# Sample rows routed ahead of the last output tile, and a new order of work up to the expert loop

## What is computed

```
x  <- LN1(alpha*x + y @ w_out)                    y: the two gated branches, merged
aff = sigmoid(x @ w_router)                       16 experts in 4 groups of 4
group g = argmax over groups of the sum of its two best (aff + b_router)
eid = the two best experts of group g;  wts = aff[eid] / sum(aff[eid])
h   = silu(xs @ w_gate[e]) * (xs @ w_up[e])       xs: the tokens of expert e, D_EXPERT = 512
x  <- LN2(alpha*x + sum over the two experts of wts * (h @ w_down[e]))
```

## Time and profile before

| | |
|---|---|
| median of 3 runs | 1908.78 us (1908.35 to 1909.92) |
| profiled execution, span | 1907.2 us |
| PE busy | 1856.5 us (97%) |
| DVE, ACT, POOL busy | 1164.8, 917.4, 481.8 us |
| w_out's last matmul ends | 1407.98 us |
| first round of the expert loop | 1462.02 us |

### The profile page before, as it was taken

One profiled execution on the slowest core, in us unless ns is written; L12 is line 12 of the kernel. 1 busy time (PEld: TensorE's weight loads), 2 busy tenths in 40 slices (PEclk: granted clock), 3 DMA queues, 4 the chain that ended last, 5 costly groups with the idle time before them and its releaser, 6 DMA issues.

```text
span 1907.2 us, 31779 instructions
## 1 busy us (share of the span) xinstructions
PE 1856.5 (97%) x11644; PEld 1663.7 (87%) x11645; DVE 1164.8 (61%) x1628; ACT 917.4 (48%) x1536; POOL 481.8 (25%) x643
## 2 busy tenths in 40 slices
PE   8999999999999999999999999999989999999997
PEld 8999988899999988889888898998857888888884
DVE  5544355642212359998999989644467587644756
ACT  3243330211210358888888888311123576645755
POOL 0000000000000215555555554002111244322333
PEclk9999999999999979999999999999988999999998
DMA  5234252232313410000000000524254798877865
GB/s 173 82 109 120 78 173 56 67 113 89 113 52 86 133 31 1 1 2 1 2 2 1 2 2 12 173 72 174 83 211 159 276 393 293 293 280 238 317 225 189
DMA packets 113735, 232.60 MB, mean 122 GB/s; under 512 B 25034, under 2 KB 81906, under 8 KB 107442
## 3 DMA queue, kind: packets, MB, share of 16 engines
q1 hardware_dynamic: 106162, 205.81, 30.5%
q0 software_dynamic: 7456, 25.17, 5.2%
HBM read 190.33 MB, written 42.71 MB: 122 GB/s over the span
## 4 chain that ended last, share of the span: by engine, by line
PE 53%; DVE 4%; ACT 3%; issue 1%; POOL 1%; DMA 0%; ACTq 0%; POOLq 0%; DVEq 0%
PE ps L3020 20%; PE ps L2069 6%; PE ps L2048 5%; PE ps L2690 5%; PE ps L254 4%; PE ps L2023 3%; PE ps L2025 3%; PE ps L3008 1%; DVE small L2133 1%; PE ps L2015 1%; PE ps L3069 1%; ACT turned_high L2238 1%; PE ps L2074 1%; PE ps L2676 1%; ACT region_w L2227 1%
## 5 line engine op out<-in xcount | busy, mean ns | idle before, releaser
L2133 DVE TENSOR_REDUCE small<-ps 128x1 f32<-128x640 f32 (+7 forms) x256 | 179.8, 703 | 26.3 <-PE ps L2015 24.4
L2157 DVE TENSOR_TENSOR turned_low<-ps,turned_high 128x512 fp32r<-128x512 f32 (+2 forms) x304 | 176.6, 614 | 12.0 <-ACT turned_high L2238 8.4
L2312 POOL TENSOR_SCALAR region_w<-region_w,small,gates 128x640 f32<-128x640 f32 (+7 forms) x172 | 141.7, 834 | 131.5 <-DVE small L2137 131.5
L2238 ACT CAST turned_high<-ps 128x512 fp32r<-128x512 f32 (+2 forms) x304 | 155.0, 531 | 31.6 <-PE ps L2048 28.2
L2023 PE MATMUL ps<-key_stacks,query_stacks 128*128 128x256 f32 (+3 forms) x384 | 142.0, 370 | 15.9 <-ACT region_w L2227 8.7
L2069 PE MATMUL ps<-turned_high,value_stacks 128*128 128x256 f32 (+1 forms) x608 | 152.1, 286 | 0.0
L2069 PE MATMUL ps<-turned_low,value_stacks 128*128 128x256 f32 (+1 forms) x608 | 142.2, 279 | 0.0
L2227 ACT ACTIVATE region_w<-ps,small 128x640 f32<-128x640 f32 (+7 forms) x172 | 121.7, 708 | 24.8 <-DVE small L2133 20.1
L3020 PE MATMUL ps<-gate_parts,rows_parts 128*128 128x512 f32 x552 | 131.7, 394 | 0.0
L3020 PE MATMUL ps<-down_parts,hidden_parts 128*128 128x512 f32 x552 | 131.1, 393 | 0.0
L3020 PE MATMUL ps<-up_parts,rows_parts 128*128 128x512 f32 x552 | 128.9, 389 | 0.0
(11 more groups left out here) (507 smaller groups left out, 4978.0 us busy)
## 6 DMA issues: line engine op xcount, KB each, us to landing
region_k<-in_w_gate SPq DMA_DIRECT2D x16, 2048.0 KB, 9.6
region_k<-in_w_up SPq DMA_DIRECT2D x16, 2048.0 KB, 10.1
region_w<-in_w_down SPq DMA_DIRECT2D x16, 2048.0 KB, 12.7
region_w<-in_w_in SPq DMA_DIRECT2D x16, 512.0 KB, 4.3
small<-gate_a SPq DMA_DIRECT2D x8, 516.0 KB, 3.4
region_w<-gate_b SPq DMA_DIRECT2D x8, 516.0 KB, 3.8
region_k<-in_x_prompt SPq DMA_DIRECT2D x8, 512.0 KB, 8.1
region_k<-in_w_in SPq DMA_DIRECT2D x8, 512.0 KB, 4.4
```

What stands on the lines that cost most here:

```text
L2133: nc.vector.tensor_reduce(nmax[:, n % 4:n % 4 + 1], sc, AX.X, ALU.max, negate=True).then_inc(s_max, 1)
L2157: nc.vector.tensor_tensor(lo, m.ps[:, turn_bank(G), 0:w], hi, ALU.subtract).then_inc(s_lo, 1)
L2238: nc.scalar.copy(hi, m.ps[:, turn_bank(G), 0:w]).then_inc(s_hi, 1)
L2312: nc.gpsimd.tensor_scalar(probs(H, t), probs(H, t), rec[:, H % 4, t:t + 1], m.gates[:, 2 * p + t, col:col + 1], ALU.mult, ALU.mult).then_i ...
```

## The change

In `output_and_router`:

- The order of the tiles is now 0 to 6, the sample rows, tile 7 (`OUT_ORDER`), and "i" counts places in this order. `choose` runs three times: tiles 0 to 5, tile 6, and tiles 7 and 8 at the end.
- Step 0's rows come from the first seven tiles alone (`EARLY`): the counting of them (`count_first`) and finding (`find_first`) are put between the matmuls of tile 7, `place_first` between those of DVE, and the gather (`gather_first`) into POOL's list.
- Tile 7 is routed from its residual z, before its norm is done: `turn` waits for the residual only, `route` multiplies with `wz` = w_router times ln1's gain, less its column mean, and one DVE operation (`logits`) scales the result by the reciprocal deviation and adds an offset from ln1's bias. For that two loads bring ln1_g and ln1_b as columns, DVE makes `wz` and the column sums (`weigh_router`, `centre_router`), and PE sums them over partitions. `scaled(TT)`, the end of tile 7's norm, comes after the last `choose`.
- If expert 0 has fewer than 128 pairs in the first seven tiles, the free places stay empty (`hole`).

In `route_experts_and_combine`:

- `count` sums per tile and rank in PSUM (10 bf16 matmuls), so `place_pairs` reads places from there; slots are counted in rows and rounded to 128 with a large constant added and subtracted. NSTEP is 34 instead of 32.
- The weights of pairs are found with float32 matmuls in one part (`values_f`) instead of a high and a low one; the table's rows come from two columns that PE turns (`table_columns`, `turn_table`).
- PE's list: step 0's products are split in passes over gate and up, with the searches, the turn of step 1's rows and `gate(1)` between them. The padding is one block of 14 instead of 12, 12 and 8.
- Step 0's turned rows have a buffer of their own (`xT_first`). SP issues w_down after the last x1 tile as before, ln2_b next, and ln2_g after `up(0)`'s products.

```diff
-NSTEP = NE + (NPAIR - 1) // P
+NSTEP = NE + (NPAIR + P - 1) // P + 1
+OUT_ORDER = (*range(TT - 1), TT, TT - 1)
+EARLY = TT - 1
...
@@ output_and_router, SP
+            for column, row in ((ro.gain_c, "ln1_g"), (ro.bias_c, "ln1_b")):
+                sp.dma_start(column, io[row].rearrange("l (k p) -> p (l k)", p=P)).then_inc(s_c, 16)
...
@@ output_and_router, POOL
-        for t in range(NT9):
-            if t + 2 < NT9:
-                high_y(t + 2)
+        for i in range(NT9):
+            if i + 2 < NT9:
+                high_y(i + 2)
...
+            if i == EARLY:
+                gather_first()
...
@@ output_and_router, PE
             for k in range(KT):
-                if t == TT and k == 2:
-                    route(t - 2)
+                if i == EARLY and k == 2:
+                    ro.route(pe, i - 2)
+                if i == EARLY and k == 4:
+                    ro.turn(pe, i - 1)
+                if i == EARLY and k == 6:
+                    ro.route(pe, i - 1)
+                if i == TT and k == 3:
+                    count_first()
+                if i == TT and k == 6:
+                    find_first()
...
@@ output_and_router, DVE
+        dve.wait_ge(s_c, 80)
+        weigh_router()
+        for i in range(EARLY):
+            if i == 4:
+                centre_router()
+            residual(i)
+            moments(i)
+            centred(i)
+            scaled(i)
...
+        choose(nc, dve, m, rs, 0, EARLY - 1)
+        dve.wait_ge(s_aff, EARLY)
+        choose(nc, dve, m, rs, EARLY - 1, EARLY)
+        residual(EARLY)
+        moments(EARLY)
+        place_first()
+        centred(EARLY)
+        scaled(EARLY)
+        keep_first()
+        keep_hole()
+        residual(TT)
+        moments(TT)
+        dve.wait_ge(ro.s_t, NT9)
+        centred(TT)
+        logits(TT)
         dve.wait_ge(s_aff, NT9)
-        choose(nc, dve, m, rs, TT - 1, NT9)
+        choose(nc, dve, m, rs, EARLY, NT9)
+        scaled(TT)
...
@@ route_experts_and_combine, SP
-        sp.wait_ge(rs.s_turned, TT)
-        sp.dma_start(gain, io["ln2_g"].rearrange("l d -> (l d)").partition_broadcast(P)).then_inc(s_c, 16)
+        sp.wait_ge(ro.s_t, NT9)
+        sp.wait_ge(rs.s_x1_out[1], 16 * 2 * (NT9 - EARLY))
         sp.dma_start(bias, io["ln2_b"].rearrange("l d -> (l d)").partition_broadcast(P)).then_inc(s_c, 16)
         load(GATE, 1)
         load(UP, 1)
+        sp.wait_ge(s_u, 1)
+        sp.dma_start(gain, io["ln2_g"].rearrange("l d -> (l d)").partition_broadcast(P)).then_inc(s_c, 16)
...
@@ route_experts_and_combine, PE
             for j in range(2 * NT9):
-                out = m.ps[:, 7, 64:64 + 2 * NSTEP].rearrange("p (v s) -> p v s", v=2)
-                last = nc.tensor.matmul(out, lanes[:, j, :], values[:, 1:3, j, :],
+                last = nc.tensor.matmul(m.ps[:, 7, 64:64 + NSTEP], lanes[:, j, :].bitcast(F32), values_f[:, j, :],
...
-        keep_awake(12)
-        count()
-        find_first()
-        keep_awake(12)
+        ro.turn(pe, EARLY)
+        pe.wait_ge(rs.s_erow, 1)
+        ro.route(pe, EARLY)
+        ro.turn(pe, TT)
+        ro.route(pe, TT)
         turn_rows(0)
-        first_products(m.ps[:, 0, :], wg, GATE).then_inc(s_g, 1)
-        first_products(m.ps[:, 1, :], wu, UP).then_inc(s_u, 1)
+        count(0, EARLY)
+        count(EARLY, NT9)
+        first_pass(GATE, 0)
+        first_pass(UP, 0)
+        keep_awake(14)
+        find_rows()
+        first_pass(GATE, 1)
+        turn_table()
+        first_pass(UP, 1)
+        turn_rows(1)
+        first_pass(GATE, 2).then_inc(s_g, 1)
         find_weights()
-        turn_rows(1)
-        turn_hidden(0)
-        keep_awake(8)
         pe.wait_ge(s_table, 1)
         gate(1)
+        first_pass(UP, 2).then_inc(s_u, 1)
+        turn_hidden(0)
...
@@ route_experts_and_combine, DVE
-        place_first()
         place_pairs()
         place_lanes()
         rows_low(0)
-        low(GATE, 0)
         keep_rows()
-        low(UP, 0)
+        table_columns()
+        low_halves(GATE, 0, (0,))
+        make_table()
+        low_halves(GATE, 0, (1,))
         weigh_pairs()
+        rows_low(1)
+        low(GATE, 1)
+        low_halves(UP, 0)
+        low(UP, 1)
+        low(DOWN, 0)
         hidden(0)
-        make_table()
-        keep_weights()
+        hidden_low(0)
```

More of the change, by code:

```diff
@@ L2661, in turn, with find_first @@
+        def find_first():
+            pe.wait_ge(rs.s_elanes, 1)
+            for t in range(EARLY):
+                last = nc.tensor.matmul(found, rs.early_lanes[:, t, :], rs.token_b[:, t, :],
+                                        start=(t == 0), stop=(t == EARLY - 1), skip_group_check=True)
+            last.then_inc(rs.s_efound, 1)
+        for i, t in enumerate(OUT_ORDER):
             n = rows_of(t)
-            pe.wait_ge(s_x1, t + 1)
-            if t >= 1:
-                pe.wait_ge(s_tk, t)
+            if i >= 2:
+                pe.wait_ge(s_z, i - 1)
+            pe.wait_ge(s_yl, i + 1)
@@ L2665, in turn @@
             for k in range(KT):
-                last = nc.tensor.transpose(m.ps[:, 4 + k // 4, (k % 4) * P:(k % 4) * P + n],
-                                           x1[t][:, k * P:(k + 1) * P], m.ident[0:n, 0:n])
-            last.then_inc(s_t, 1)
-        def route(t):
-            n = rows_of(t)
-            pe.wait_ge(s_tk, t + 1)
-            if t >= 2:
-                pe.wait_ge(s_aff, t - 1)
-            for k in range(KT):
-                last = nc.tensor.matmul(m.ps[0:n, 6 + t % 2, 0:NE], x1T[:, k, 0:n], wr[:, k, :],
-                                        start=(k == 0), stop=(k == KT - 1))
-            last.then_inc(s_r, 1)
@@ L2785, in route_experts_and_combine @@
     tmp = take(2 * NQ)
-    upto, pos = take(NQ), take(NQ)
-    rank0, upto0 = (take(NT9) for _ in range(2))
+    pos = take(NQ)
     nt, T, Tex = (take(NE) for _ in range(3))
-    more = take(NE * NKX)
-    slot, steps, lane = (take(2 * NT9) for _ in range(3))
-    wt, w_low = take(2 * NT9), take(2 * NT9)
+    cnt = take(1)
+    late = take(NT9)
+    slot, lane = (take(2 * NT9) for _ in range(2))
+    wt, first_slot = take(2 * NT9), take(2 * NT9)
     filled = take(NSTEP)
-    w_part = take(NSTEP)
     weights = take(NSTEP)
-    tabf = take(2 * NSTEP + 2)
+    ended, begun, columns = take(NE), take(NE), take(2)
     mark_in, mark_out = take(1), take(1)
@@ L2869, in last_three, with turned_rows @@
         return a, a + 1, a + 2
+    def turned_rows(s):
+        return xT_first if isinstance(s, int) and s == 0 else xT
     def banks(b, n):
@@ L3193, in _ @@
         act.wait_ge(s_table, 1)
-        body(1)
+        high(GATE, 1)
+        keep_weights()
+        high(UP, 1)
+        high(DOWN, 0)
+        hidden_high(0)
+        gated(1)
         n = steps_of(act)
@@ L3271, in place_pairs @@
[L3271 to L3273 removed]
+            dve.wait_ge(s_cnt, 1)
+            dve.wait_ge(rs.s_estep, 4)
+            total = ranks[:, NT9, :]
+            step(tt(cnt[:, 0:1], total[:, 0:1], rs.hole, ALU.add))
+            ts(nt[:, 0:1], cnt[:, 0:1], P / 2 - 0.5, ROUND, ALU.add, ALU.add).then_inc(s_v, 1)
+            ts(nt[:, 1:NE], total[:, 1:NE], P / 2 - 0.5, ROUND, ALU.add, ALU.add).then_inc(s_v, 1)
@@ L3283, in place_pairs @@
-            tt(values[:, 0], chosen, bc(rs.token.unsqueeze(2), pairs), ALU.mult)
+            step(ts(nt, nt, -ROUND, float(P), ALU.add, ALU.max))
+            nc.vector.tensor_tensor_scan(T, rs.ones[:, 0:NE], nt, 0.0, ALU.mult, ALU.add).then_inc(s_v, 1)
+            ts(late, ranks[:, 0:NT9, 0], rs.early_end, rs.hole, ALU.is_ge, ALU.mult).then_inc(s_v, 1)
+            done[0] += 2
+            dve.wait_ge(s_v, done[0])
+            step(tt(Tex, T, nt, ALU.subtract))
+            at = pos.rearrange("p (t e) -> p t e", e=NE)
```

513 lines of the change are left out of this document (307 added, 206 removed).

## The result

The changed kernel takes 1900.2 us (median of 4 runs, 1898.9 to 1900.65), the kernel before 1909.35 us beside it (1908.35 to 1910.87): a ratio of 0.995, 95% interval 0.9939 to 0.9962, so 9.2 us faster. Forecast were 1901.2 and the range 1897.5 to 1905.5. The profiled execution has a span of 1898.9 us, 8.3 less than that of before.

What follows compares the result with a forecast made beforehand. TensorE, 97% busy, bounds; only w_out to expert loop gives time. `up(1)` at 1429.8 + 22.2 + 2.0 + 0.4 = 1454.4, 7.6 earlier: span 1899.6, median 1.6 above, 1901.2 us; range 1897.5 to 1905.5.

Steps and rivals of the forecast that it cites:

- F: End of `find_rows`, the search for step 0's rows: forecast 1429.8, bounds 1428.8 to 1431.5, 1439.42 in the kernel before.
- w_out's end: End of the last w_out matmul: 1408.4 instead of 1407.98, with interleaved counting and finding matmuls estimated at 0.4 us.
- Column loads: ln1_g and ln1_b loads ahead of the x rows: constants arrive at 1302.2 to 1305.6, PE stalls 0 to 1.3, 0.4 taken.
- The last choice: Final `choose` after tile 7's `route`: starts 1414.1 to 1414.7, 1414.7 taken, 1.4 us earlier, takes 3.8, ends 1418.5.
- 16 products, padding: PE after the last choice: 16 high-part products 5.7 us, to 1424.65, then 14 padding matmuls to 1427.9, so DVE isn't late.
- F to up(1): From the end of `find_rows` to the loop's first `up(1)`: 22.2 us, including 1.0 for loop entry, before the clock's cost.
- The clock: Low granted clock somewhere in F+9 to F+18, around `find_weights`: costs 0 to 3.4 us, 2.0 taken.
- A: Rival, warm: PE keeps 2.4 GHz from F on; 2.0 us less, 1899.2; chance 0.17.
- B: Rival: clock also falls at step 1's gather wait, or w_down's load delays that gather; 2 to 4 us, 1904; chance 0.20.
- C: Rival: after F, DVE slips and `find_weights` runs at half clock throughout; 5 us more, 1906; chance 0.08.
- D: Rival, slower: the 4-byte column loads hold up tile 0's norm until 1315.7; 1913; chance 0.03.
- E: Rival: seven tiles can't fill step 0, expert 0 gets holes, perhaps one more round of 17.74 us; chance under 0.01.

Runs made afterwards that it cites:

- after_again: The changed kernel, unedited, run and profiled once more; 1899.75 us against 1910.34 for the kernel before, ratio 0.995.
- columns_x4: The changed kernel with each of the two ln1 column loads issued four times; 1900.74 us against 1911.1 for the kernel before, ratio 0.995.
- slow_places: The changed kernel with three useless DVE operations of 0.8 us ahead of `place_pairs`; 1904.03 us against 1910.34 for the kernel before, ratio 0.9969.
- late_gather: The changed kernel with step 0's row gather waiting for the last choice, count before turn, padding out; 1909.48 us against 1908.4 before, ratio 1.0002.
- both_undone: The changed kernel with tile 7 routed from its finished norm, step 0's gather behind the last choice, padding out; 1912.84 us, ratio 1.0016.

## Why the prediction was right

The time was 1.0 below the forecast. The path up to the loop came as it was laid out, its price of the clock did not: `up(1)` was expected at 1454.4 (at 1452 to 1456 among the signs) and started at 1451.65, just ahead of that (it was cold and took 1.6 more, so 2.75 earlier at its start is 1.2 earlier at its end), and the 22nd round was expected 7.6 earlier and came 8.3 earlier. That nearness is in part luck: in after_again the 22nd round starts at 1822.97, 11.6 earlier, because w_out started earlier and no low stretch came after F. The medians are the better measure: 9.2 us gained for 7.6 forecast. Step by step:

- **w_out's end**: 1408.4 expected, 1408.27 came. That it hits the instant is luck, as this end lies up to 3 us later in other executions. But counted from w_out's first matmul (1291.18 before, 1290.91 now) the end comes 0.56 later, for the 0.4 that the interleaved work was costed at.
- **Column loads**: 0 to 1.3 us with 0.4 taken, 0 came. The price was too high: I bounded it by the rates in the earlier trace rows, 320 and 674 runs a microsecond, which is what the queue moved then, not the most it can. columns_x4 showed some 1590. The rule of the Trainium skill ("DMA: Bandwidth & Descriptors", Rules for kernel authors) that I weighed there agrees on the count: the whole execution has 27114 packets under 512 B where the kernel before has 25034, 2080 more. On the price, which that rule doesn't state, the trace decides: the load cost nothing here.
- **The last choice**: forecast 1414.7 to 1418.5, came 1414.65 to 1418.45. I had allowed for the clock falling in `route`, and it did, 3.02 us; in after_again it was 1.97 and the choice 1.1 earlier after w_out's end.
- **16 products, padding**: 5.7 and 3.25 expected, 5.26 and 3.04 came. `place_pairs` took 5.1 (1419.64 to 1424.7) for an estimated 5.0. F was forecast at 1429.8 (1428.8 to 1431.5) and came at 1429.04.
- **F to up(1)**: 22.2 without the clock's share; 1451.65 - 1429.04 = 22.6 came. Inside, the wait for the gather was 1.15 (expected 1.65), `find_weights` 4.21 (expected 3.8, from `route`'s 0.21 a matmul; it came at 4.21 / 18 = 0.234), `gate(1)` 5.55, the pass of up 1.85, the idling before the turn 0.85 and "issue" 0.99 (expected 1.0). The entry gap was a guess between 0 and ACT's 1.5, as PE showed none in the trace of before; it was right in size.
- **The clock**: this step failed, and that the sum still came out is luck. 2.0 us were to be lost in F+9 to F+18, in or after `find_weights`. Nothing was lost there (the clock was 1.00 from 1435 to 1452); instead 1.05 went in `route` (which lay within the allowance of the choice's start) and 1.6 in the first `up(1)`. The sum came out within a microsecond because a low stretch of about the forecast size lay at another place. slow_places shows that my place can be hit, after_again that in another execution neither is. I argued from one execution of before, and the cold stretches of one execution are not a property of the kernel. What could be forecast was that one or two stretches of 3 to 7 us would be at half clock and cost 0 to 3.4; that their place could be named was more than the trace carried.

The rivals: **A** (warm) is the state of after_again's profile (its span of 1895.6 is below the 1899.2 - 1.6 = 1897.6 that A means); **B** didn't come in either profile of the change: nothing was lost at the gather of step 1, which took 4.36 us in after_again, where 4.98 was assumed (late_gather's slow gather met mostly tile 7's stores); **C** (gain given back) and **D** didn't come; **E** didn't either, the rounds are 17.76 and 22 and more of them as before.

What decided the case was shown by the undoing: without the residual's route F is 6.9 later, without the early gather 7.3 later, without both the kernel is slower than before.

## What to carry to other kernels

A long serial chain between two dense stretches is shortened by starting each piece from the earliest value that suffices (here the residual instead of the norm, seven tiles instead of nine), and the worth of each such piece is read by undoing it alone and then with the others, since they share what hides them. Where an engine waits for a short operation and then enters a loop, keep a few of its matmuls back for both moments: it made the stage 2.0 us shorter here, and the padding nothing that could be measured. Profile two executions before naming the place where the clock falls, and give its cost a range rather than a place.

## What the runs showed of the hardware

- 6144 more runs of 4 bytes delayed a load's arrival by 4.2 us; 3173 such packets moved in 2 us on SP's queue, 1590 a microsecond, where I had taken 674 as the best rate.
- A gather of 128 rows took 4.67, 4.98 and 7.26 us with 0.28, 0.91 and 1.39 MB of SP's transfers in the same time (both_undone, before, late_gather). Three executions, not a controlled series: what moved beside it differed in kind too.
- A float32 matmul of 34 columns took 0.234 us (4.21 for 18), an fp32r one of 68 columns 0.122 (2.20 for 18).
- The granted clock fell in the first `up(1)` in one profiled execution of the changed kernel and not in the other, with the same gaps ahead of it to within 0.01 us; the fall cost 1.6 us, one in `gate(1)` together with the search 3.2 us (4.74 + 8.42 against 4.21 + 5.72).
